# A transformer pair on one core: the lower parts of the FFN down weights made by a negative copy and an accumulating DMA

## The reference, cut to what matters

```python
def swiglu_ffn(h, w_in, w_out):
    gate, up = jnp.split(h @ w_in, 2, axis=-1)
    return (jax.nn.silu(gate) * up) @ w_out
# first block:  x = x + swiglu_ffn(rms_norm(x), w_ffn_in, w_ffn_out)                         -> fa
# second block: x = x + 0.5 * swiglu(rms_norm(x), ffn1_gate, ffn1_up, ffn1_down)             -> fb
#               ... mixer, cross attention ...
#               x = x + 0.5 * swiglu(rms_norm(x), ffn2_gate, ffn2_up, ffn2_down); rms_norm   -> fc
```

## Time and profile before

| what | us |
|---|---|
| median of 3 runs (lowest, highest) | 2385.22 (2384.91, 2385.42) |
| the profiled execution's own time | 2385.45 |
| span of its trace, from first to last instruction | 2383.6 |
| PE busy | 2359.7 |
| DVE busy | 1525.4 |
| ACT busy | 1167.8 |
| POOL busy | 266.8 |

### The profile page before, as it was taken

How to read it: one execution, slowest core, us unless ns; L and a number is a source line. 1 busy time by engine, 2 the same in 40 slices (tenths; PEclk the granted TensorE clock), 3 DMA queues, 4 the chain that set the end, 5 groups by cost and what they waited for, 6 DMA issues and landing times.

```text
span 2383.6 us, 34351 instructions
## 1 busy us (share of the span) xinstructions
PE 2359.7 (99%) x13792; PEld 2007.5 (84%) x13792; DVE 1525.4 (64%) x2207; ACT 1167.8 (49%) x1910; POOL 266.8 (11%) x210
## 2 busy tenths in 40 slices
PE   8999999999999999999999999999999999999998
PEld 7777778777888888899988899988887888899987
DVE  5688746468775465687743687753677565777742
ACT  7766664234464254455543555532644354555532
POOL 0000000455200010110002200001033201100000
PEclk9999999999999999999999999999999999999999
DMA  6221234333576231233233243233322232333231
GB/s 199 78 72 51 82 107 161 105 98 104 164 223 217 97 124 62 89 124 107 89 107 97 62 131 102 87 110 94 105 69 63 91 112 74 103 110 107 95 99 55
DMA packets 171119, 251.89 MB, mean 106 GB/s; under 512 B 9936, under 2 KB 89040, under 8 KB 170960
## 3 DMA queue, kind: packets, MB, share of 16 engines
q1 hardware_dynamic: 169808, 248.13, 32.8%
q10 hardware_dynamic: 1152, 1.57, 0.2%
HBM read 231.83 MB, written 16.78 MB: 104 GB/s over the span
## 4 chain that ended last, share of the span: by engine, by line
PE 95%; DVE 3%; ACT 1%; issue 1%; DMA 0%; POOL 0%; SPq 0%; DVEq 0%; POOLq 0%; ACTq 0%
PE bank L1349 93%; PE bank L1509 1%; DVE wlo L2314 1%; PE bank L1532 0%; DVE T L2322 0%; PE bank L1633 0%; PE bank L1657 0%; DMA zb<-scr_z 0%; DVE macc L2314 0%; PE bank L1475 0%; ACT whi L1751 0%; DMA raw<-in_w_in 0%; DVE ml L2322 0%; DVE xg L2318 0%; DVE bank L2620 0%
## 5 line engine op out<-in xcount | busy, mean ns | idle before, releaser
L2314 DVE TENSOR_TENSOR wlo<-raw,whi 128x1024 fp32r<-128x1024 f32 (+2 forms) x310 | 381.6, 1234 | 244.0 <-ACT whi L1751 243.9
L1349 PE MATMUL bank<-xopr,shi 128*128 128x256 f32 x2688 | 484.1, 283 | 0.1
L1751 ACT ACTIVATE whi<-raw 128x1024 fp32r<-128x1024 f32 (+2 forms) x310 | 318.7, 1034 | 281.2 <-PE bank L1349 274.4
L1349 PEld LDWEIGHTS bank<-xopr,shi 128*128 128x128 f32 x2688 | 419.5, 192 | 0.5 <-DVE slo L2314 0.3
L1349 PE MATMUL bank<-xh,whi 128*128 128x512 f32 x1016 | 411.5, 405 | 8.2 <-DVE wlo L2314 8.2
L1349 PE MATMUL bank<-xh,wlo 128*128 128x512 f32 x1016 | 397.9, 392 | 0.0
L1349 PE MATMUL bank<-xl,whi 128*128 128x512 f32 x1016 | 397.2, 391 | 0.0
L1349 PE MATMUL bank<-xopr,slo 128*128 128x256 f32 x1344 | 380.3, 283 | 0.0
L1349 PEld LDWEIGHTS bank<-xopr,slo 128*128 128x128 f32 x1344 | 258.0, 192 | 0.0
L1349 PEld LDWEIGHTS bank<-xh,whi 128*128 128x128 f32 x1016 | 191.5, 188 | 64.7 <-issue 20.2
L1349 PEld LDWEIGHTS bank<-xh,wlo 128*128 128x128 f32 x1016 | 191.3, 188 | 41.7
(11 more groups left out here) (380 smaller groups left out, 4230.8 us busy)
## 6 DMA issues: line engine op xcount, KB each, us to landing
raw<-in_w_in SPq DMA_DIRECT2D x92, 512.0 KB, 3.6
raw<-in_ffn_down SPq DMA_DIRECT2D x44, 512.0 KB, 3.8
quarter<-in_w_ffn_in SPq DMA_DIRECT2D x32, 512.0 KB, 4.5
quarter<-in_ffn_gate SPq DMA_DIRECT2D x32, 512.0 KB, 3.9
quarter<-in_ffn_up SPq DMA_DIRECT2D x32, 512.0 KB, 4.8
raw<-in_w_ffn_out SPq DMA_DIRECT2D x22, 512.0 KB, 3.8
raw<-in_w_xattn_kv SPq DMA_DIRECT2D x16, 512.0 KB, 4.2
raw<-in_w_kv_mem SPq DMA_DIRECT2D x16, 512.0 KB, 4.9
```

The lines of the kernel that those rows point to most:

```text
L1349: return e.matmul(out, l, r, start=start, stop=stop, skip_group_check=skip)
L1751: return e.activation(out, in_, ACT.Copy)
L2314: return e.tensor_tensor(out, a, b, op)
```

## The change

For the 66 pieces of the three down weights `wlo` is no longer made by DVE. ACT, behind its copy of `raw` to `whi`, makes a second copy `wlo = -whi`, and then POOL issues a DMA that adds `raw` to `wlo` in SBUF (`accum_op=add`, 128 rows of 1024 float32 from SBUF to SBUF). POOL issues piece i's DMA only when that of piece i-2 is complete. "w lo" of such a piece, for which PE and the loads wait, is now that DMA's completion. All other weights and the 33 products keep DVE's subtraction.

```diff
+        BY_DMA = {i for n in (f"{tag}d{i}" for tag in SEVEN for i in range(2)) for i in G[n]["ids"]}
@@ scalar, weight(i)
                 copy(whi[i % NH][:, :, 0:n], raw[i % NR][:, :, 0:n]).then_inc(*up("w_hi", ("w hi", i)))
+                if i in BY_DMA:
+                    w.wait_ge(*at("w hi", i))
+                    copy(wlo[i % NH][:, :, 0:n], whi[i % NH][:, :, 0:n].bitcast(F32), -1.0).then_inc(
+                        *up("w_hi", ("w negative", i)))
@@ vector, weight(i)
+                if i in BY_DMA:
+                    return
                 w.wait_ge(*at("w hi", i))
                 tt(wlo[i % NH][:, :, 0:n], raw[i % NR][:, :, 0:n], whi[i % NH][:, :, 0:n].bitcast(F32), ALU.subtract).then_inc(
@@ gpsimd
+            def add_weight(i):
+                if i not in BY_DMA:
+                    return
+                n = sum(x[2] for x in slots[i][0])
+                w.wait_ge(*at("w negative", i))
+                if i - 2 in BY_DMA:
+                    w.wait_ge(*at("w lo", i - 2))
+                e.dma_start(wlo[i % NH][:, :, 0:n].bitcast(F32), raw[i % NR][:, :, 0:n], accum_op=ALU.add).then_inc(
+                    *T.up("pool", f"d_added{i % 2}", (("w lo", i),), 16))
+
-            does = {"square": square, "weigh": weigh, "state": state_,
+            does = {"w_lo": add_weight, "square": square, "weigh": weigh, "state": state_,
```

## The result

The changed kernel takes **2390.2 us** in the median of 20 runs (2388.76 to 2392.33), the kernel before 2385.46 us in 20 (2384.03 to 2386.96). The ratio is 1.002, 95% interval 1.0014 to 1.0026: 4.7 us slower. That lies in the predicted range, on the predicted side, and is a third of the predicted 14.6 us. The profiled executions have spans of 2389.4 and 2383.6 us, 5.8 us apart; that of the changed kernel took 2391.18 us, 1.0 us above its median.

What follows compares the result with a forecast made beforehand. PE was taken as the bound, busy 2359.7 of 2383.6 us. Waits at first pieces and seams plus a lost clock, 3.3 + 6.7 + 2.1 + 0.1 + 2.4 = 14.6 us, gave 2400 us, range 2388 to 2440.

Steps and rivals of the forecast that it cites:

- seam of `fa`: Pieces 12 and 13 of `fa`, adding DMAs issued behind POOL's copies and six sums: PE loses 6.7 us.
- piece 0 of three stages: First piece of `fa`, `fb`, `fc`: 5.4 us of room for the adding DMA, 3.3 us lost in all.
- seams of `fb` and `fc`: Piece 13 there, behind one copy and three sums: room 4.4 and 6.4 us, cost 2.1 and 0.1 us.
- lost clock: Behind the stall at piece 13 of `fa`: 12 matmuls at 1.2 GHz cost 2.4 us more.
- What L is: Step estimating the adding DMA's time from loads of 1024 KB: 6.5 us, with ends 2.7 and 11.1.
- L: Time of an adding DMA from when POOL can issue it to its completion, taken as 6.5 us.
- DMA engines saturated: Rival: adding DMA needs over 3.86 us of all engines per piece, every piece late, 2440 us; chance 0.14.
- Hidden: Rival: adding DMA under 4.6 us, no first piece late, loss under 0.2%, 2388 to 2390 us; chance 0.15.
- Faster: Rival: relieved DVE brings evictions, norms earlier or matmuls faster; about 1 us to win, 2384 us; chance 0.03.

Runs made afterwards that it cites:

- e4: Changed kernel, but no adding DMA issued: ACT still makes the 66 negative copies, DVE waits for each and subtracts as before; 2385.13 us, ratio 0.9999.
- e8: Kernel before the change plus 45 adding DMAs into an idle buffer that nothing reads, reloads of `raw` waiting for them; 2385.17 us, ratio 0.9999.
- e3: Changed kernel with DMAs ordered straight behind the upper part and pieces 0, 1, 2 of each stage given back to DVE; 2385.2 us, ratio 0.9998.
- e5: e1 with the load of piece 4 of each stage held back until piece 1's `wlo` is made; 2385.06 us, ratio 0.9999.
- e2: Changed kernel with the first three pieces of each down weight made by DVE's subtraction again; 2387.96 us, ratio 1.0008.
- e1: Changed kernel with each adding DMA ordered straight behind the upper part, ahead of sums of the same tile; 2388.2 us, ratio 1.001.
- e9: Changed kernel with six additional POOL copies into an idle buffer ahead of piece 13's DMA in `fa`; 2395.97 us, ratio 1.0044.
- e7: e1 plus 45 additional adding DMAs into an unread buffer, so most pieces have two; 2422.36 us, ratio 1.0156.
- e10: Changed kernel with twenty additional POOL copies into an idle buffer ahead of piece 13's DMA in `fa`; 2405.43 us, ratio 1.0084.

## Why the prediction was right in kind and too large

The mechanism held in its outline: the work that DVE loses was hidden already, ACT's and the DMA engines' new work is hidden too (e4, e8), and the loss is the sum of the waits at places where an adding DMA has little room (e3, e5). But of the places that it named only the seam of `fa` cost anything, and two thirds of the loss stand at a place that it did not name. The terms went like this:

| term | predicted | measured in the trace |
|---|---|---|
| piece 0 of three stages | 3.3 | 0; piece 1 instead, 3.8 |
| seam of `fa` | 6.7 | 2.1 |
| seams of `fb` and `fc` | 2.2 | 0 |
| lost clock | 2.4 | 0 |
| sum | 14.6 | 5.8 (span), 4.7 (medians) |

**The step that failed is "What L is": one value of 6.5 us used at every place.** The 6.5 is what the trace has as its median, 6.4. But the cost is made only where room is short, and there L was mostly not the median. An adding DMA that starts on idle engines takes 4.4 to 4.8 us, one with a load issued 0.1 to 0.3 us behind it 7.0 to 7.5. Piece 0 has nothing beside it, which the prediction had itself read (share 0.00) and not used in L; it takes 4.4 to 4.6 us, under its room of 5.4, and the 3.3 us are gone. Piece 13 at the seam of `fa` has no load issued beside it, only piece 14's adding DMA behind it, and takes 4.7. At the seams of `fb` and `fc`, where a load is issued 1.6 and 1.45 us ahead of it, it takes 5.0, and the rooms were 5.3 and 6.6 us, not 4.4 and 6.4, so the 2.2 us are gone too; the first of them is a near thing, for in e2 that DMA took 5.8 us and PE waited 0.5 us.

**Not named: piece 1.** Its room is 6.1 us, more than piece 0's 5.4, so that with L = 6.5 everywhere its 0.4 us would have vanished behind piece 0's 1.1. That the end of piece 0's DMA sets free the load of piece 4 just then follows from the `load` rule in the code; the prediction followed the chain to PE and not to SP. That this load slows piece 1's DMA by 2.4 us no row of before had; e5 shows it: hold back that load, and the 3.4 us that e1 had left at the three pieces 1 are gone. The prediction had called itself wrong if PE waited somewhere unnamed, and if L was under 4.6 us; the first came true, and the second at some of the places that counted.

**The seam.** Of the forecast 6.7 us, 4.6 did not come: 1.8 because L was 4.7, and 2.8 because the DMA was issued 2.2 us earlier than forecast (the sums took 7.6 us and not 10.4, and began 0.5 later) while PE wanted the piece 0.6 later, at 1270.89. The order of POOL's work was right, and e1 shows that it was the cause: moved ahead of the last two sums (issued at 1264.75 in e1, L = 4.7) the DMA costs nothing.

**The clock.** Right in kind, as e9 shows, and charged for a stall that did not come. At the predicted stall of about 6 us it costs 1.6 us rather than 2.4; at 2.1 us nothing.

**The rules of the Trainium skill.** By the Trainium skill's page "DMA: Bandwidth & Descriptors", section "Anatomy of one DMA — SWDGE (gpsimd) path", 512 KB would land in an estimated 3.2 us; the shortest here was 4.4, so for an adding DMA the rule is too short. The Trainium skill's page "Collectives: The Full Stack", section "The bandwidth ceiling: the fold count and why AG ≠ RS ≠ AR", says of the adding step of a ReduceScatter that both of its sources have to be read through one ring; carried over to this DMA the estimate was 4.4 us, and the lone DMAs here agree (4.4 to 4.8). The sum by it was 4.6 us, close to the measured 4.7, but partly by chance: it has no piece 1 in it, and twice too much for the seam.

**The rivals.** *DMA engines saturated* is not in force, though nearer than its share of 0.29 before suggests: by the estimate of e7 a load and one adding DMA take at most about 4.0 of 5.44 us, and a second adding DMA makes every piece late (e7). The adding one takes at most about 2.5 us of the engines, under the 3.86 that the rival needed. *Hidden* had 2388 to 2390 us and came within 0.2 us of the measured time, in part by luck: its L under 4.6 us held for lone DMAs only, it put up to 4.8 us on the seam of `fa`, where 2.1 were lost, and it had nothing for piece 1. *Faster* didn't happen; with all waits removed the kernels of e3 and e5 are level with the one before (2385.2 and 2385.06 us), as the 8.2 us of the earlier trace rows had said: none of them beats it.

Open: why eight matmuls are slow behind the gap of e9 and twelve behind that of e10; and how a load and an adding DMA share the engines so that the adding one, which came first, loses 2.4 us to a load 0.3 us behind it, and hardly anything (5.0 us) to a load 1.5 us ahead of it.

## What to carry to other kernels

When work moves from an engine to an asynchronous transfer, don't price the transfer by its median: list the places with the shortest room, and price it there, with what runs beside it at that moment. Look above all at what the transfer's own completion releases, since that starts exactly when the next one needs the engines; holding that load back for a few microseconds was free here. And put the issue of a transfer that someone waits for ahead of work on the issuing engine that nobody waits for.

## What the runs showed of the hardware

**DVE was held up for 7.6 us while POOL ran its sums.** At the seam of `fa` POOL's six sums took 11.9 us in the kernel before and 7.6 after. I had put any such gain down to DVE's missing subtractions. DVE's timeline of the changed kernel, and the line for its `xl` there (count, shortest, median and longest in ns), say otherwise:

```profile
1260.60 0.67 DVE L2319 TENSOR_TENSOR xT<-xT,bank 128x512 f32<-128x512 f32 x1
1261.44 8.28 DVE L2327 SCALAR_TENSOR_TENSOR xl<-xT,gboth,xh 128x512 fp32r<-128x512 f32 x2 [0.17 <-ACT xh L1753]
```
```profile
L2327 DVE SCALAR_TENSOR_TENSOR xl<-xT,gboth,xh x4: 739/849/7620, 1258.4 to 1269.0; 128x512 fp32r<-128x512 f32 x4
```

An `xl` that otherwise takes 0.74 us stands from 1261.44 to 1269.06, ending 0.56 us after POOL's last sum (1267.04 and 1.46 us). The same happens in e8, where DVE still makes every `wlo`, but POOL has a DMA to issue just ahead of its sums; in e4, without such a DMA, it does not, and the sums take 10.9 us (the line of e8, then that of e4):

```profile
L2326 DVE SCALAR_TENSOR_TENSOR xl<-xT,gboth,xh x4: 739/824/7595, 1256.2 to 1267.6; 128x512 fp32r<-128x512 f32 x4
```
```profile
L2327 DVE SCALAR_TENSOR_TENSOR xl<-xT,gboth,xh x4: 740/1041/1783, 1256.9 to 1264.1; 128x512 fp32r<-128x512 f32 x4
```

In e1, where that DMA has moved away from the head of the sums and the next stands behind four of them, the longest `xl` is 1.38 us, though DVE's subtractions are missing there too. So a DMA's issue right ahead of the sums, and not the missing subtractions, goes with the held DVE instruction and six quick sums. That the issue lets the sums queue up and follow each other without a gap in which DVE could get in is my reading; no run shows it. The Trainium skill, page "SBUF — State Buffer", section "Who interferes with whom", has a DVE instruction with two SBUF inputs contend with GpSimd's reads, and the later of the two blocked until the other's instruction ends. The trace agrees that DVE is blocked; that it stays so over some five POOL instructions in a row, and not one, goes beyond what the page says. Nobody waited for this `xl`, so it cost nothing here.

**Smaller ones.** POOL is busy for 0.86 us in the median with the issue of such a DMA (0.85 to 1.37). A load of 512 KB that shares the engines with an adding DMA lands about 1 us later in the median (3.8 to 4.8).
